# Norm work taken chunk by chunk, and a new order of steps in the cross attention of a two-layer decoder

## The reference

```python
h = rmsnorm(x, norm_mix);  proj = h @ w_in             # then MLA, GLA and pooling heads
x = x + mix @ w_out
# cross attention: 4 heads of 256; the prompt sees its own memory, each sample a cache of its own
q = rmsnorm((rmsnorm(x, norm_xa) @ w_xq).reshape(B, T, 4, 256), g_xq)
p = softmax(einsum('bthd,bnhd->bhtn', q, mem_k) / 16)
x = x + einsum('bhtn,bnhd->bthd', p, mem_v) @ w_xo
x = x + square(relu(rmsnorm(x, norm_mlp) @ w_ff1)) @ w_ff2
```

## Time and profile before

| | |
|---|---|
| median of three runs | 1376.51 us |
| the profiled execution | 1374.13 us, of which 1372.4 us from first to last instruction |
| TensorE busy | 1256.8 us (92%) |
| VectorE, ScalarE, GpSimd busy | 833.7, 496.1, 191.5 us |
| mean granted TensorE clock | 0.958 |
| moved by DMA | 250.4 MB, 182 GB/s over the span |

### The profile page before, as it was taken

One profiled execution on the slowest core, in us unless ns is written; L12 is line 12 of the kernel. 1 busy time (PEld: TensorE's weight loads), 2 busy tenths in 40 slices (PEclk: granted clock), 3 DMA queues, 4 the chain that ended last, 5 costly groups with the idle time before them and its releaser, 6 DMA issues.

```text
span 1372.4 us, 24013 instructions
## 1 busy us (share of the span) xinstructions
PE 1256.8 (92%) x9292; PEld 1116.1 (81%) x9292; DVE 833.7 (61%) x1366; ACT 496.1 (36%) x848; POOL 191.5 (14%) x337
## 2 busy tenths in 40 slices
PE   4989989979988789999989899999899887999998
PEld 4966767759986589999989677667699856999998
DVE  5566675775764557664465667657666555766442
ACT  4232323253331336553342323232443313556431
POOL 1242522400000000000012533225000000000000
PEclk9989999979999899999999999999999988999999
DMA  8624655743474735554565257448345664455552
GB/s 319 223 62 144 215 170 147 216 153 123 154 299 186 282 123 185 178 184 168 185 222 193 76 164 227 139 139 253 142 152 214 246 275 164 149 183 182 184 185 93
DMA packets 75088, 250.40 MB, mean 182 GB/s; under 512 B 11440, under 2 KB 44544, under 8 KB 54368
## 3 DMA queue, kind: packets, MB, share of 16 engines
q1 hardware_dynamic: 58896, 194.05, 40.5%
q0 software_dynamic: 13968, 47.57, 10.8%
q10 hardware_dynamic: 2112, 7.26, 1.4%
...
## 4 chain that ended last, share of the span: by engine, by line
PE 75%; DVE 11%; ACT 5%; issue 4%; DMA 3%; POOLq 1%; POOL 0%; DVEq 0%; ACTq 0%
PE ps L1313 47%; PE ps L1322 17%; DMA big<-in_pages 2%; DVE area L718 2%; PE ps L1589 2%; DVE ring_r L697 2%; ACT qkA_r L435 1%; PE ps L1736 1%; PE ps L1328 1%; DMA ring<-in_units 1%; ACT sq L435 1%; DVE ssn L994 1%; PE ps L1759 1%; DMA xT<-in_xt 1%; PE ps L1548 1%
## 5 line engine op out<-in xcount | busy, mean ns | idle before, releaser
L1322 PE MATMUL ps<-wuq_b,latT 128*128 128x260 f32 x1024 | 254.6, 398 | 12.9 <-ACT sc L435 10.9
L1313 PE MATMUL ps<-qkA_r,ring_r 128*128 128x264 f32 x880 | 254.8, 290 | 0.0
L1322 PEld LDWEIGHTS ps<-wuq_b,latT 128*128 128x128 f32 x1024 | 194.1, 195 | 59.2 <-issue 13.9
L1313 PEld LDWEIGHTS ps<-qkA_r,ring_r 128*128 128x128 f32 x880 | 170.8, 194 | 0.0
L363 POOL DMA_DIRECT2D big<-in_pages x256 | 138.5, 541 | 229.2 <-issue 213.2
L1313 PE MATMUL ps<-big_r,ring_r 128*128 128x264 f32 x512 | 145.5, 284 | 0.0
L697 DVE TENSOR_TENSOR ring_r<-ring,latT_r 128x2048 fp32r<-128x2048 f32 x42 | 96.3, 2292 | 59.3 <-ACT latT_r L435 58.6
L435 ACT ACTIVATE latT_r<-ring 128x2048 fp32r<-128x2048 f32 x42 | 80.4, 1914 | 138.8 <-DMA ring<-in_units 138.8
L1313 PE MATMUL ps<-qkA_r,latT_r 128*128 128x264 f32 x320 | 96.5, 302 | 22.3 <-DVE xg_r L706 20.0
L1313 PE MATMUL ps<-xg_r,latT_r 128*128 128x264 f32 (+1 forms) x384 | 112.3, 293 | 0.0
L435 ACT ACTIVATE qkA<-ps 128x512 f32<-128x512 f32 x86 | 51.1, 594 | 161.1 <-PE ps L1322 160.9
...
## 6 DMA issues: line engine op xcount, KB each, us to landing
ring<-in_units SPq DMA_DIRECT2D x136, 1024.0 KB, 4.9
big<-in_pages POOLq DMA_DIRECT2D x256, 144.0 KB, 3.4
latT<-in_pages SPq DMA_DIRECT2D x256, 128.0 KB, 2.7
big<-in_units SPq DMA_DIRECT2D x16, 1024.0 KB, 8.8
...
xg<-in_memt POOLq DMA_DIRECT2D x2, 1024.0 KB, 6.3
out_mk<-latT ACTq DMA_DIRECT2D x2, 1024.0 KB, 3.9
out_mv<-latT ACTq DMA_DIRECT2D x2, 1024.0 KB, 7.8
```

Source lines behind the costliest of these rows:

```text
L1313: ins = mm(out, a(i, k), b(j, k), start=first and k + n == 0, stop=last and k == KD - 1 and n == 2)
L1322: ins = mm(out, a, b, start=i == 0, stop=i == len(pairs) - 1)
```

## The change

It has two parts and some small edits.

**Chunks.** `x_part` is sent after each residual add. ScalarE makes a chunk's high half and its square right then (`x_parts`), VectorE its low half and a running sum in `rB`, two chunks behind the adds; four squares are in flight in `y`. `mean_x` follows the first result tile and not the first unit. For layer 2's first norm this goes on during the last products of layer 1's MLP, and layer 2's gains are copied there. At the very start the chunks follow one another.

**Cross attention.** The query's gain goes onto the prompt's keys (ScalarE, eight copies) and onto the samples' query as it is put into `hot`; the root of the query norm goes into the exponent's scale and onto the maxima, as nine columns (two for each head of the prompt, one for the samples), so z is not scaled. The sums are products with one column. The samples' keys come first, in the order 0 to 7, though they are still loaded in the order 6, 7, 0, 4, 1, 5, 2, 3; then the scores of all four heads. Values are loaded and used from 0 to 7. The output's halves are made head by head, and the high halves of the output projection's units lie in other buffers.

**Small.** A reciprocal of 528 columns is cut in two parts at neighbouring places, and the memory's sum of squares is three adds and no reduce.

The diff, cut to its core:

```diff
-MEMORY_ORDER = (6, 7, 0, 4, 1, 5, 2, 3)
+KEYS_LOADED = (6, 7, 0, 4, 1, 5, 2, 3)
...
-          12: (2, 0), 14: (2, 2), 13: (2, 3), 15: (2, 6), 16: (2, 7), 17: (3, 1), 19: (3, 2), 20: (3, 3), 21: (3, 6), 22: (3, 7),
+          12: (2, 0), 14: (2, 2), 13: (2, 3), 15: (2, 6), 16: (2, 7), 17: (3, 0), 18: (3, 1), 19: (3, 2), 20: (3, 3), 21: (3, 6), 22: (3, 7),
...
-        hi_xo = [within(latT_rf, 0, UNIT), within(sq_rf, 0, UNIT), within(z_rf, 0, UNIT), within(qkA_rf, 0, UNIT)]
+        hi_xo = [within(latT_rf, 0, UNIT), within(z_rf, 0, UNIT), hi_mix[0], hi_mix[1]]
...
                 def load_memory(part, first):
-                    for b in MEMORY_ORDER:
+                    for b in range(B) if part else KEYS_LOADED:
...
# ScalarE
+            def x_high(k, g):
+                act.wait_ge(sems["x_part"], at["x_part"].free())
+                f(hi_x[:, k, :], xT[:, k, :], ACT.Copy, scale=gain[:, g + k:g + k + 1]).then_inc(sems["op_hi"], 1)
+            def x_square(k):
+                act.wait_ge(sems["sq_used"], at["sq_used"].free())
+                f(x_sqs[k % 4], xT[:, k, :], ACT.Square).then_inc(sems["x_sq"], 1)
...
-                split_units(2, hi_xq)
                 act.wait_ge(sems["km_ready"], l + 1)
...
-                square_x(G_XA)
+                x_parts((0, 1), G_XA)
+                split_units(1, hi_xq)
+                x_parts((2, 3), G_XA)
+                split_units(1, hi_xq)
+                x_parts((4, 5, 6, 7), G_XA)
+                power(P, T)
                 split_units(U_XQ - 2, hi_xq)
                 at["unit_used"].next(U_XK + U_XV - WIDE)
+                act.wait_ge(stored, 16 * STORES * (l + 1))
+                for i in range(KD):
+                    last = f(kmT[:, i, :], kmT[:, i, :], ACT.Copy, scale=gain[:, G_XQ + i % 2:G_XQ + i % 2 + 1])
+                last.then_inc(sems["xk_ready"], 1)
...
+                split_heads((0, 1))
                 split_units(2, hi_xo)
+                split_heads((2,))
                 act.wait_ge(sems["xo_ready"], l + 1)
-                split_operand(hi_out, mix)
+                f(hi_out[:, :, TP:T], mix[:, :, TP:T], ACT.Copy).then_inc(sems["op_hi"], 1)
+                split_heads((3,))
                 split_units(2, hi_xo)
...
# VectorE
+            def x_sum(k):
+                wait("x_sq")
+                if k:
+                    step(v.tensor_tensor(rB[:, :], x_sqs[0] if k == 1 else rB[:, :], x_sqs[k % 4], ALU.add))
+                    dve.sem_inc(sems["sq_used"], 2 if k == 1 else 1)
+                if k == KD - 1:
+                    tell("ssum_ready")
...
                     add_to_x(k)
+                    if k >= 2:
+                        x_parts((k - 2,), G_XA)
+                x_parts((6, 7), G_XA)
                 tell("x_new")
...
                 step(v.memset(hot, 0.0))
+                for h in range(H):
+                    step(v.tensor_tensor(hot_diag[h], z[:, 2 * h:2 * h + 2, TP:T],
+                                         gain[:, G_XQ:G_XQ + 2].unsqueeze(2).broadcast_to([P, 2, B]), ALU.mult))
+                tell("hot_q")
                 wait("xq_stat")
-                step(v.tensor_scalar(m[:, 0:T], ps[:, 5, 0:T], 1 / 256, EPS, ALU.mult, ALU.add))
-                refine(P, T)
-                tell("head_root")
-                head_scales(z, z, G_XQ, T)
-                tell("xq_ready")
+                step(v.tensor_scalar(of_query[1], ps[:, 5, 0:9], 256 * EPS, None, ALU.add))
+                tell("d_moment")
...
# TensorE
-                    if i == 0:
-                        mean_x()
+                        if i + a == 0:
+                            mean_x()
...
+                def query_sums(h):
+                    wait("xq_sq")
+                    for a in range(2):
+                        product(ps[:, 5, 2 * h + a:2 * h + a + 1], [(sq[:, 2 * h + c, P * a:P * a + P], ones[:, 0:1]) for c in range(2)])
+                    for c in range(2):
+                        ins = mm(ps[32 * h:32 * h + B, 5, 8:9], sq[:, 2 * h + c, TP:T], ones[:, 0:1], start=False, stop=True,
+                                 skip_group_check=True)
+                    return ins
...
-                raw_scores((0, 1))
                 wait("hot_q")
                 t = bank()
-                for b in MEMORY_ORDER:
+                for b in range(B):
                     u = memory_unit(0, b).rearrange("p (h c n) -> p h c n", h=H, c=2)
                     for c in range(2):
                         if c == 1:
                             settle()
...
-                ready(ins, True)
+                ready(ins, True, "wide_used")
+                query_sums(H - 1).then_inc(sems["xq_stat"], 1)
+                raw_scores((0, 1))
                 raw_scores((2, 3))
-                turned((0, 1))
...
+                turned((0, 1))
                 wait("x_t")
                 attended((0, 1))
-                turned((2, 3))
...
                 wait("hot_p")
-                sample_values(MEMORY_ORDER[:4])
+                sample_values(range(SLOTS))
+                turned((2, 3))
+                sample_values(range(SLOTS, B)).then_inc(sems["xv_sum"], 1)
...
                 wait("x_t")
-                attended((2, 3))
-                sample_values(MEMORY_ORDER[4:]).then_inc(sems["xv_sum"], 1)
+                attended((2,))
                 wait("xs_out")
...
-                wait("xo_ready")
-                mixed(hi_xo)
+                attended((3,))
+                mixed(hi_xo, None, (7, 0, 0, 0, 0, 0, 1, 1))
```

207 lines of the change are left out of this document (136 added, 71 removed).

## The result

The changed kernel took 1336.24 us (median of 4 runs, 1329.92 to 1340.65) beside 1376.88 us of the kernel before (1371.6 to 1378.96): a ratio of 0.971, interval 0.966 to 0.976. Its profiled execution took 1340.65 us, with a span of 1339.0. The 40.6 us are the forecast's 41.5 (1376.5 to 1335). The total was right; how it is made up was not in every part, as the experiments show. Medians in this document are over all runs of a kernel; ratios, clocks and means are over its fast runs alone, that is without the few that lie more than 1.5% above its fastest.

The account below looks back on a forecast made before the run. TensorE bounds it, busy 92%; only its 116 us of standing and its lower clock can be won. 2 x (14.3 + 3.6) + 4.6 + 0.7 - 0.8 = 40.3 off 1374.1 gives 1333.8, called 1335; range 1326 to 1344.

Parts of the forecast that it names:

- Entries: Starts of projections behind the residual adds: chunks win 3.5 us at the query's, 3.6 at the MLP's, 4.6 into layer 2.
- the 0.7 an entry: Fixed extra time of small chunks, if on the path at five entries: gain 3.5 us smaller; held to be hidden.
- Cross attention: From second query unit to output projection, 69.0 us for 77.0; with the faster projection and entry, 14.3 won a layer.
- the case that I had named and not taken: Samples' keys: were the clock low at 421, the 2.2 us stall before key 3 would cover it.
- signs of being wrong: Pauses over 1 us inside projections, one over 3 before the output projection, or clock under 0.8 through keys and scores.
- signs of being right: `xg_r` wait near 14.1, no 4.1 reduce, keys within 4 us, one key 3 stall, gapless scores, output projection 11.5 earlier.
- The start: Kernel's very start: mean ahead of the second tile pauses TensorE some 3.6 us; 0.8 lost, bounds 0.5 gain, 2 loss.
- The small edits: Memory's sum of squares as three adds: 0.7 us won once; reciprocal cut in two: 0, between 3 won and 1 lost.
- A higher clock: Rival: clock stays high in attended pair, late unit and entries, 10 us more won, 1325 us; chance 0.10.
- a lower one: Rival: attention stays at the lower clock behind its pauses, 16 us in all, 1351 us; chance 0.21.
- Stalled units: Rival: chunks on ScalarE and VectorE hold up weight units, so TensorE waits; 1452 us, or 1393 with half; chance 0.03.
- nothing is won: Rival: the waits only move to the root and the evictions, 1374 us; chance 0.04.

Follow-up runs that it names:

- e0: The changed kernel run once more, nothing altered, as the mark for the other runs: 1337.41 us, 0.973 of the kernel before.
- e5: Changed kernel with the old norm at the five entries (all adds, then whole-array square and one reduce, mean behind the second tile): 1365.67 us, 0.993 of the kernel before.
- e1: Changed kernel with all eight adds first, then the eight chunks, and the mean behind the second tile: 1380.18 us, 1.005 of the kernel before.
- e11: Changed kernel with 7, 7 and 4 useless products filling three pauses of cross attention, no wait removed: 1332.65 us, 0.969 of the kernel before.
- e9: Changed kernel, two heads' scores before the keys, four values before the attended pair, first output unit split earlier, layer 1's first mean behind the second tile: 1314.58 us, 0.958.
- e7: Changed kernel with the memory's squares summed in one reduction and the reciprocal in one instruction again: 1336.14 us, 0.972 of the kernel before.
- e2: Changed kernel with the scores of heads 0 and 1 moved ahead of the samples' keys: 1317.34 us, 0.958 of the kernel before.
- e3: Changed kernel with the first four cached values moved ahead of the turned shares and the attended pair: 1326.46 us, 0.964 of the kernel before.
- e8: Kernel before with only the changed kernel's chunked norm, cross attention left as it was: 1360.90 us, 0.992 of the kernel before.

## Why the prediction was right, point by point

**What bounds it.** Right: none of what was saved is TensorE's work (1255.2 for 1256.8 busy); 31.8 of the 33.4 us between the two spans are standing time. Incomplete: I had priced the waits, and the low clock only for the attended pair and the late output projection. Beside e0 at most 10.6 of the 36.0 us gained are low clock that went.

**Entries.** 3.5, 3.6 and 4.6 us were forecast. From the end of the last product before to the second unit, layer 1's query entry took 8.3 us for 10.5, layer 2's 7.6 for 10.5; the MLP's 7.1 for 10.5 and 7.1 for 10.6; layer 2's 6.7 for 10.9. So 2.1 and 2.9, 3.4 and 3.5, 4.2: 16.2 for the forecast's 18.8. Half of what is missing are late chunks. I had only chunk 7 late, by 0.4 at four entries; TensorE waits 1.24 for three of them at layer 1's query entry and 0.3 to 0.7 at the others, 2.9 in all, since VectorE's pitch for low part and sum is 0.98 and TensorE wants a chunk each 0.37. Against that stands a gain that I had not seen: the earlier chunks let ScalarE go earlier too, and the wait for the first query square, forecast at 1.7, is 0.50 (1.34 in e5, with the old norm).

**The rule on small tiles.** The Trainium skill ("VectorE: DVE Perf Modes", section on the TRN2 errata) advises tiles of 512 elements or more, because of a fixed cost of each instruction. The trace agrees on the fixed part: VectorE's additions of 1024, 512 and 256 columns (the memory's sum of squares) take 1.22, 0.69 and 0.42 us, from which I estimate 0.15 that does not depend on the size. Where nothing covers it, the same chunks, late, are 14.5 us dearer than the bulk form of e5 (1380.18 and 1365.67). But the price is not the 0.7 an entry that I named: TensorE even stands less in e1 than in e5 (98.0 and 104.6 us); fed in small pieces, it runs the entries at the low clock. In the changed kernel the chunks lie under products, and they pay. I had held the cost hidden, and it is, but only through the overlap.

**Cross attention.** 69.0 us were forecast from the second query unit to the output projection, for 77.0; it took 71.2 in layer 1 and 71.0 in layer 2 (77.0 and 77.8 before). The order of events came as told, each mark a little late: keys 422.6 (421.2), keys' end 432.1 (430.4), scores' end 440.3 (438.9), attended pair's end 454.0 (451.2), output projection 467.2 (464.3). Terms that were off: the third query unit, 3.4 us of it at the low clock (1.7 lost), in this profile alone; the keys at the low clock, with a stall of 0.65 for 2.2, which is the case that I had named and not taken, and e11, with the keys at the full clock, measured the other, 1.88; the attended pair, 6.3 for 5.4. The wait for the second output unit (3.56 in the earlier trace rows) is gone, and the output projection ran in 23.7 for 23.5. Of my signs of being wrong none came; of the signs of being right two were missed, the stall before key 3 (0.65 and 0.91, told as 1 to 3) and the start of the output projection, 8.6 earlier for 11.5.

**The start.** 0.8 us lost was forecast. The mean ahead of the second tile left 3.39 us idle and the tile behind it at the low clock, and yet the unit behind the small products at 46 to 48 us starts only 0.24 later (48.05 for 47.81): up to there the loss is smaller than told. By 72 us the loss is 1.8, since the clock is low from 57.1 to 60.5. It is low there in e9 too, where the mean is back at its old place, so it does not need this pause; what brings it stays open.

**The small edits.** 0.7 was forecast for the memory's sum, 0 for the reciprocal; e7 finds neither, and 0.7 is less than it can show.

**The sum.** In the pair of profiles, 33.4 us apart by their spans, the entries are 16.2 (forecast 18.8), and the attention with its output projection 12.5 + 5.0 = 17.5 (forecast 2 x (8.0 + 2.9) = 21.8): 33.7 for 40.6. The other stages cancel: 0.6 won ahead of layer 1's query entry, 1.8 in its MLP and 0.5 in the last one, 3.3 lost ahead of cross attention in layer 2 (below). So of the two main terms 14% and 20% did not come. That the total of the medians, 1336.24, is within 1.3 us of 1335 is in part luck: the changed kernel's profile is the slowest of its four runs, and the medians are 40.6 apart.

One assumption that no sentence of the forecast spoke out did fail: that the two parts add up. The sum gave 21.8 us to the attention and 18.8 to the norm. By the table, the attention alone is worth 9.2 and the norm alone 10.4; the remaining 16.4 come only when both are there, and nearly all of them are in the rest, the time at the lower clock. A forecast made for one of the parts by this sum would have been about twice too high.

**Not of the change.** The stage ahead of cross attention in layer 2 took 358 to 370 us in the profiles of the same code, and its clock lay between 0.94 and 0.97. The changed kernel's profile has a stretch of 12 us there with TensorE busy throughout and a clock of 0.63; another kernel with the same code in that stage had 1.00 (windows of 12 us, first the changed kernel):

```profile
880.00:892.00 12.00, 12.00 (x40) 7.70 (x39) 4.45 (x14) 1.73 (x6) 2.81 (x6) 0.63 0.44 136
```

The same window of e7:

```profile
880.00:892.00 12.00, 12.00 (x59) 9.06 (x58) 5.39 (x16) 2.40 (x8) 3.54 (x7) 1.00 0.52 167
```

The low clock lasts from 883.1 to 896.8 and costs up to 7 us; stretches of the same length without a pause stand in the profiles of e0, e1, e2, e3, e5, e8 and e9 too, two of them in e3 and e8, and none in the kernel before. The spread of a kernel's runs is the clock: beside e0 the kernel before took 1362.14 us at 0.969 and 1388.22 at 0.947, which is 1320 and 1315 as time x clock. How much of it such stretches make is not shown. One profile against another is no evidence for less than 7 us.

**The rivals.** A higher clock (1325) and a lower one (1351) both stayed out. Stalled units did not come: behind their entries the projections of the stretch have no pause over 1 us inside. That nothing is won was wrong from the first run on. In e8 more than a third of what the norm gives in time x clock (16.7 us) is lost again by a longer time at the low clock (6.3).
